# Factors of the output multiplied out in the input projection, and a two-step finish of the head tiles on GpSimd

## What is computed

```
xm, o_pre = split(x @ w_in)                    # 2 x 2048 wide
xc = silu(causal_dwconv(xm, conv_w, conv_b))   # width 4
q, k = headwise(xc, w_q), headwise(xc, w_k);  v = headwise(xm, w_v)
h, C, n, m = mlstm_cell(q, k, v, gates, C, n, m)
hn = (h - mean(h)) * rsqrt(var(h) + eps)       # over the 512 values of a head
out = sigmoid(o_pre) * (hn * norm_g + skip * xc)
y = out @ w_down
```

## Time and profile before

| what | value |
|---|---|
| median of 3 runs | 3442.8 us (3435.66 to 3448.84) |
| the profiled execution | 3447.66 us, of which its span 3446.1 us |
| mean granted TensorE clock | 0.972 of full speed |
| busy, share of the span | TensorE 93%, VectorE 42%, ScalarE 24%, GpSimd 24% |
| projection, loop of it | 1300 to 1650 us |
| score loops of heads 0 to 3 | 1755 to 1876, 1943 to 2067, 2134 to 2258, 2323 to 2443 us |
| down projection | from 2458 us |

### The profile page before, as it was taken

The page is one execution under the profiler, slowest core; times in us unless marked ns, Lnnn a source line. Parts: engine busy times, 40 slices in busy tenths (PEclk is TensorE's granted clock), DMA queues, the critical chain, the costliest instruction groups (busy, mean ns, idle before and its releaser), DMA issues.

```text
span 3446.1 us, 53547 instructions
## 1 busy us (share of the span) xinstructions
PE 3210.0 (93%) x21153; PEld 2934.7 (85%) x21153; DVE 1439.9 (42%) x2086; ACT 813.7 (24%) x1526; POOL 810.4 (24%) x519
## 2 busy tenths in 40 slices
PE   6999899999999989999688879897799999999996
PEld 5777689999999979999476767676799999999995
DVE  2001444333333353433456574748524533333334
ACT  3101532111111151111424233333202311111113
POOL 2112033333323213322001010101232333333320
PEclk9999999999999999999799999999899999999998
DMA  7544211111111104232435353525711111111111
GB/s 214 132 116 111 81 50 50 50 43 49 43 49 43 43 25 175 101 116 81 154 124 205 118 180 132 185 87 186 262 44 44 49 44 49 43 49 43 49 31 51
DMA packets 275684, 318.22 MB, mean 92 GB/s; under 512 B 23577, under 2 KB 215337, under 8 KB 274322
## 3 DMA queue, kind: packets, MB, share of 16 engines
q1 hardware_dynamic: 255289, 250.27, 23.7%
q10 hardware_dynamic: 12960, 40.04, 3.0%
q0 software_dynamic: 7296, 25.96, 2.1%
HBM read 224.88 MB, written 92.19 MB: 92 GB/s over the span
## 4 chain that ended last, share of the span: by engine, by line
PE 82%; DVE 9%; ACT 4%; issue 3%; DMA 2%; SPq 0%; DVEq 0%; ACTq 0%; POOL 0%; POOLq 0%
PE ps L366 22%; PE ps L367 21%; PE ps L368 21%; PE ps L1784 3%; PE ps L1039 2%; PE ps L1002 2%; PE ps L1014 1%; PE ps L1011 1%; PE ps L984 1%; ACT X L448 1%; PE ps L1012 1%; PE ps L1097 1%; DVE DN L1433 1%; PE ps L387 1%; DVE RST L435 1%
## 5 line engine op out<-in xcount | busy, mean ns | idle before, releaser
L366 PE MATMUL ps<-AH,WH 128*128 128x352 f32 x3072 | 1001.7, 326 | 10.3 <-DVE AL L2241 6.2
L367 PE MATMUL ps<-AL,WH 128*128 128x352 f32 x3072 | 987.5, 321 | 0.0
L368 PE MATMUL ps<-AH,WL 128*128 128x352 f32 x3072 | 987.3, 321 | 0.0
L353 POOL TENSOR_SCALAR WH<-RAW 128x1024 fp32r<-128x1024 f32 x200 | 233.0, 1165 | 1748.2 <-PEq L373 1676.5
L366 PEld LDWEIGHTS ps<-AH,WH 128*128 128x128 f32 x3072 | 578.7, 188 | 36.7 <-issue 23.5
L367 PEld LDWEIGHTS ps<-AL,WH 128*128 128x128 f32 x3072 | 580.1, 189 | 0.9
L368 PEld LDWEIGHTS ps<-AH,WL 128*128 128x128 f32 x3072 | 578.0, 188 | 0.0
L355 POOL TENSOR_TENSOR WL<-RAW,WH 128x1024 fp32r<-128x1024 f32 x200 | 506.5, 2533 | 16.7
L366 PE MATMUL ps<-HH,WH 128*128 128x352 f32 x1536 | 500.4, 326 | 0.0
L367 PE MATMUL ps<-HL,WH 128*128 128x352 f32 x1536 | 493.6, 321 | 0.0
L368 PE MATMUL ps<-HH,WL 128*128 128x352 f32 x1536 | 493.2, 321 | 0.0
(11 more groups left out here) (290 smaller groups left out, 3640.0 us busy)
## 6 DMA issues: line engine op xcount, KB each, us to landing
RAW<-in_ffn_w SPq DMA_DIRECT2D x128, 512.0 KB, 3.6
CT<-in_state_mlstm_C SPq DMA_DIRECT2D x32, 1024.0 KB, 5.5
out_C_s<-CT SPq DMA_DIRECT2D x32, 1024.0 KB, 4.6
RAW<-in_ml_w_in SPq DMA_DIRECT2D x32, 512.0 KB, 3.8
RAW<-in_conv_w_pw SPq DMA_DIRECT2D x24, 512.0 KB, 7.4
STK<-u_scratch SPq DMA_DIRECT2D x48, 190.0 KB, 3.5
xc_scratch<-XC ACTq DMA_DIRECT2D x16, 528.0 KB, 2.7
so_scratch<-SO ACTq DMA_DIRECT2D x16, 528.0 KB, 3.7
```

The source lines that it names most:

```text
L353: pool.tensor_scalar(WH[:, k % 4], RAW[:, k % 2], 1.0, 0.0, ALU.mult, ALU.add).then_inc(w_hi, 1)
L366: pe.matmul(ps[:, bank, 0:CW], wh[:, k, cols], hi[:, k, cs], start=(k == 0), stop=False)
L367: pe.matmul(ps[:, bank, 0:CW], wh[:, k, cols], lo[:, k, cs], start=False, stop=False)
L368: mm = pe.matmul(ps[:, bank, 0:CW], wl[:, k, cols], hi[:, k, cs], start=False, stop=(k == nk - 1))
```

## The change

`gate_sigmoid` becomes `silu_tile`: ScalarE applies Silu to XC in place, and VectorE's product goes. A new `out_factors` on VectorE then makes ZT = XC * skip * SO, in one operation, and SO = SO * norm_g in another. It stands in VectorE's queue ahead of the taps of the next tile. `spill_tile` waits for both and writes ZT to a new scratch array too: five DMAs, ahead of XC's. With these, out = hn * (norm_g * SO) + ZT, so `gain` goes, and `finish` is a product and a sum of whole tiles of four feature tiles each (128 x 1024), without a choice of column. GpSimd does it for chunks 0, 1 and 2, and for DEC and END of a head at the start of the next; those of head 3 stay on VectorE. `xo_load` reads ZT's array in place of XC's.

The diff, cut to its core:

```diff
-        def gate_sigmoid(act, j, s):
+        def silu_tile(act, j, s):
             wait(act, mtaps, 8 * j + 8)
-            wait(act, xc_done, j)
-            act.activation(SGX[:], XC[:, s], ACT.Sigmoid).then_inc(sgx_done, 1)
+            act.activation(XC[:, s], XC[:, s], ACT.Silu).then_inc(xc_done, 1)
 
         def spill_tile(act, j, s):
 
             wait(act, xc_done, j + 1)
-            wait(act, so_done, 3 * j + 3)
+            wait(act, z_done, j + 1)
+            act.dma_start(ZS[j], ZT[:]).then_inc(spill[s], 16)
             act.dma_start(XCS[j], XC[:, s]).then_inc(spill[s], 16)
...
+        def out_factors(dve, j, s, stored):
+
+            wait(dve, xc_done, j + 1)
+            wait(dve, so_done, 3 * j + 3)
+            wait(dve, spill[1 - s], stored)
+            dve.scalar_tensor_tensor(ZT[:], XC[:, s], PRM[:, j, 6:7], SO[:, s], ALU.mult, ALU.mult)
+            dve.tensor_scalar(SO[:, s], SO[:, s], PRM[:, j, 5:6], None, ALU.mult).then_inc(z_done, 1)
+
         def phase_a_dve(dve, i, first):
             for s in range(2):
                 j = 2 * i + s
+                if not (first and s == 0):
+                    out_factors(dve, j - 1, 1 - s, 0 if first else 80 * i)
                 dve.wait_ge(xm_put, 4 if first and s == 0 else 3 * j + 3)
...
-                dve.wait_ge(mtaps, 8 * j + 8)
-                dve.wait_ge(sgx_done, j + 1)
-                dve.tensor_tensor(XC[:, s], XC[:, s], SGX[:], ALU.mult).then_inc(xc_done, 1)
...
-            for m, src in enumerate((XCS, SOS)):
+            for m, src in enumerate((ZS, SOS)):
...
+            if not (isinstance(h, int) and h == 0):
+                finish(pool, h - 1, DEC)
+                out_store(pool, h - 1, DEC)
             xo_load(pool, h, 1)
             if not (isinstance(h, int) and h == 0):
+                finish(pool, h - 1, END)
                 out_store(pool, h - 1, END)
...
             vm(4)
+            finish(pool, h, 0)
             out_store(pool, h, 0)
             vm(5)
             xo_load(pool, h, 2)
             vm(6)
+            finish(pool, h, 1)
             out_store(pool, h, 1)
             vm(7)
             xo_load(pool, h, 3)
+            finish(pool, h, 2)
             out_store(pool, h, 2)
             xo_load(pool, h, 4)
-            out_store(pool, h, DEC)
...
-                finish(dve, h - 1, DEC)
...
-            if not first:
-                finish(dve, h - 1, END)
...
-                    if n == 6:
-                        skip(dve, h, tc)
-                    if n == 7:
-                        gate(dve, h, tc)
...
-        def finish(dve, h, tc):
-            skip(dve, h, tc)
-            gate(dve, h, tc)
-
-        def skip(dve, h, tc):
+        def finish(eng, h, tc):
+
+            def absorb():
+                if not isinstance(h, int):
+                    eng.sem_inc(steps_seen, 1)
             w = TC[tc][1]
...
             x = HT[tc % 2][:, :, 0:w]
+            eng.wait_ge(xo_in[tc % 2], (96, 64)[tc % 2] * h + 32 * (tc // 2 + 1))
+            absorb()
+            eng.wait_ge(hnorm, 5 * h + tc + 1)
+            absorb()
+            eng.tensor_tensor(x, x, XO[tc % 2][:, 1, :, 0:w], ALU.mult).then_inc(hskip, 1)
+            eng.wait_ge(hskip, 5 * h + tc + 1)
+            absorb()
+            eng.tensor_tensor(x, x, XO[tc % 2][:, 0, :, 0:w], ALU.add).then_inc(hout, 1)
...
             pool.wait_ge(upd_mm, 4 * DEC_B * HEADS)
+            out_store(pool, HEADS - 1, DEC)
             pool.wait_ge(o_out[1], 16 * 8)
...
-            gain(act, HEADS - 1, DEC)
             down_high(0)
...
+            out_factors(dve, NJ - 1, 1, 80 * NJ // 2)
             dve.wait_ge(t_g, 1)
```

More of the change, by code:

```diff
@@ L270, in program @@
         ma_mm, xm_put, so_done, km_done = sem("ma_mm"), sem("xm_put"), sem("so_done"), sem("km_done")
[L271 removed]
+        gate_mm, gs_put, ge_ev, mtaps, z_done, xc_done = sem("gate_mm"), sem("gs_put"), sem("ge_ev"), sem("mtaps"), sem("z_done"), sem("xc_done")
         mhist_put = sem("mhist_put")
@@ L295, in program @@
         den_abs, den_div, num_ev = sem("den_abs"), sem("den_div"), sem("num_ev")
-        hmean, hcent, hsq, hvar, hsd, hrst, hnorm, hgain, hskip, hout = [sem("h" + x) for x in
-                                                                        ("mean", "cent", "sq", "var", "sd", "rst", "norm", "gain", "skip", "out")]
+        hmean, hcent, hsq, hvar, hsd, hrst, hnorm, hskip, hout = [sem("h" + x) for x in
+                                                                        ("mean", "cent", "sq", "var", "sd", "rst", "norm", "skip", "out")]
         chunk_in = [sem(f"chunk_in{c}") for c in range(3)]
@@ L815, in phase_a_act @@
                 act.wait_ge(gate_mm, j - 1)
-                act.wait_ge(spill[s], 64 * i)
+                act.wait_ge(spill[s], 80 * i)
                 act.sem_inc(steps_seen, 1)
@@ L833, in phase_a_dve @@
                     dve.wait_ge(gate_mm, j - 1)
-                    dve.wait_ge(spill[s], 64 * i)
+                    dve.wait_ge(spill[s], 80 * i)
                 hist = mdec(XM[:, s, MHIST + SEQ:XW], 7)
@@ L1150, in root @@
             act.activation(SD[:, 0:w], ps[:, 7, 256:256 + w], ACT.Sqrt, bias=eps[:]).then_inc(hsd, 1)
-        def gain(act, h, tc):
-            w = TC[tc][1]
-            act.wait_ge(hnorm, 5 * h + tc + 1)
-            if not isinstance(h, int):
-                act.sem_inc(steps_seen, 1)
-            for vt in range(VT):
-                x = HT[tc % 2][:, vt, 0:w]
-                ins = act.activation(x, x, ACT.Copy, scale=PRM[:, hd(h, vt), 5])
-            ins.then_inc(hgain, 1)
         def phase_b_act(act, h, first):
@@ L1179, in phase_b_act @@
                     root(act, h - 1, DEC)
-                if not first and x == 14:
-                    gain(act, h - 1, DEC)
             if first:
@@ L1202, in phase_b_act @@
                     act.activation(DDR[:], DDR[:], ACT.Exp, bias=CC[0:NDEC, 8, bass.ds(h, 1)]).then_inc(ddec, 1)
-                if i == 3 and not first:
-                    gain(act, h - 1, END)
             def high(q):
@@ L1235, in phase_b_act @@
                         root(act, h, tc)
-                    if n == 6:
-                        gain(act, h, tc)
                 if q + 1 < NS:
@@ L1585, in _ @@
             sp.dma_start(NRW[:], a["state_mlstm_n"][0].rearrange("b h (v p) -> (b h v) p", p=P)).then_inc(s_m0, 16)
-            sp.wait_ge(spill[0], 16 * 4 * 8)
-            sp.wait_ge(spill[1], 16 * 4 * 8)
+            sp.wait_ge(spill[0], 16 * 5 * 8)
+            sp.wait_ge(spill[1], 16 * 5 * 8)
             sp.dma_start(XCH[:], inner_tiles(XCS, 0)).then_inc(ld_xc, 16)
@@ L1712, in _ @@
             pool.memset(QZ[:], 0.0).then_inc(s_neg, 1)
-            pool.wait_ge(spill[0], 16 * 4 * 8)
-            pool.wait_ge(spill[1], 16 * 4 * 8)
+            pool.wait_ge(spill[0], 16 * 5 * 8)
+            pool.wait_ge(spill[1], 16 * 5 * 8)
             pool.wait_ge(w_free, NP_A + 32)
@@ L2119, in _ @@
             down_high(1)
-            gain(act, HEADS - 1, END)
             down_high(2)
@@ L2318, in _ @@
             dve.wait_ge(e_cc, 1)
-            dve.wait_ge(spill[0], 16 * 4 * 8)
-            dve.wait_ge(spill[1], 16 * 4 * 8)
+            dve.wait_ge(spill[0], 16 * 5 * 8)
+            dve.wait_ge(spill[1], 16 * 5 * 8)
             block_weights(dve, 0)
```

20 lines of the change are left out of this document (5 added, 15 removed).

## The result

The changed kernel took 3456.76 us (median of 8 runs, 3452.7 to 3460.97); the kernel before took 3443.4 us on the same chip (8 runs, 3435.66 to 3448.84). The ratio is 1.0039, 95% interval 1.0028 to 1.0051: slower by 0.4%, less than the 0.5% that was called within reach of a measurement, but well outside the interval, and 20.8 us above the forecast of 3436.0 and just outside its range.

What follows compares the result with a forecast made beforehand. TensorE was taken as full in the projection; in the score loop TensorE and VectorE wait for each other. Terms +1.1 - 3.2 + 1.6 - 4.5 - 1.8 make -6.8 us: 3436.0 us against the median, range 3420 to 3455.

Steps and rivals of the forecast that it cites:

- The projection: Input projection: added products, fifth store and table loads are covered while TensorE is fully busy; 0 us.
- Rival C: Input projection: ScalarE's table loads are exposed, up to 20.5 us; +13.7 us in all, 3456.5 us; chance 0.04.
- Behind the last tile: After the last projection tile: gate values GE wait for two products and five DMAs; +1.1 us.
- Chunk 0: Score loop, four heads: GpSimd's product delays PL by 0.8 us, less 1.6 for the skip; -0.8 us each.
- Rival B: Chunks 0 and 1: GpSimd's two products back to back shut VectorE out of both; 3451.6 us without clock loss; chance 0.17.
- Chunk 1: Score loop, four heads: mean of PL first (-1.0) and PL late (+1.8); +0.4 us each.
- the late outcome: Chunk 1: PL waits for GpSimd's first product, DN for its second operation; +1.8 us.
- Chunk 2: Score loop: the skip is followed by a 2.40 us wait for TensorE's scores, so nothing to gain; 0 us.
- Between heads: Head turns: gate leaves VectorE's queue, -3.3 us; gain and DEC's finish go from in front of VL, -1.2 us.
- The tail: After the last head: DEC keeps its finish on VectorE but without the gain; -1.8 us.
- its costlier half: Rival B with TensorE's clock halving behind longer waits, about 1.5 us in each of eight places: 3463.6 us; chance 0.09.

Runs made afterwards that it cites:

- e4: The changed kernel with GpSimd's product and sum of chunks 0 and 1 moved one mask later (behind VM 5 and VM 7): 3464.92 us, ratio 1.0059.
- e2: The kernel before plus two idle differences on GpSimd, which read SBUF, in chunks 0 and 1 of each head: 3464.05 us, ratio 1.0053.
- e3: The kernel before plus five idle fills on GpSimd, which read no SBUF operand, in chunks 0 and 1: 3448.01 us, ratio 1.0003.
- e9: The changed kernel with GpSimd's product of chunks 0 and 1 ahead of the mask, sum behind it, chunk 1's sum also awaiting DN: 3433.24 us, ratio 0.9965.
- e8: The changed kernel with six idle instructions ahead of VectorE's loop over the heads: 3462.6 us, ratio 1.0060.
- e1: The changed kernel with product and sum of every chunk, DEC and END on VectorE, GpSimd keeping stores and loads: 3452.5 us, ratio 1.0027.
- e5: e1 with eight idle instructions on VectorE ahead of its head loop: 3439.58 us, ratio 0.9995.
- e7: e5 with only chunk 2, DEC and END finished by GpSimd: 3436.92 us, ratio 0.9980.
- e12: The kernel before with only the last tile's XC store ahead of gate values GE, its other stores behind the row computations: 3444.64 us, ratio 1.0003.

## Why the prediction was wrong

**The projection, 0: right.** TensorE is busy 342.00 of 342.00 us, two products and a fifth store included. The load of a table on ScalarE:

```profile
1506.83 1.28 ACT L763 ACT_TABLE_LOAD   x1
1508.12 1.08 ACT L763 ACTIVATE XC<-XC 128x1056 f32<-128x1056 f32 x1
1510.16 0.46 ACT L782 COPY XM<-ps 128x352 f32<-128x352 f32 x1 [0.96 <-PE ps L369]
```

The Silu follows its load at once, and the wait behind it fell from 2.38 us to 0.96, by about one load. Rival C is out. The price of some 2.66 us a switch that the Trainium skill gives ("ScalarE: Activation LUTs", section "What ACT_TABLE_LOAD costs") doesn't hold here: a load is 1.28 us, and the Silu starts 0.01 us behind it.

**Behind the last tile, +1.1: mis-sized,** +1.9. GE comes 6.4 us behind the Silu where it came 4.6 behind the Sigmoid, +1.8. ZT took 1.32 and SO 0.77 us, as assumed (1.26 and 0.8); the five stores held ScalarE for 4.29 us, from 1650.61 to 1654.90, where 3.58 were assumed.

**Chunk 0, -0.8 each: this step failed,** with +1.8, +2.5, +2.5, +1.5. The mechanism was named (a product of GpSimd shuts VectorE's out for its length), and its price per product was right: 2.37 us on GpSimd, 2.6 to 2.8 on VectorE. What was wrong was what stands there. The prediction saw PL alone, caught by the first product, and the sum beside PSUM readers. But PS stands ahead of PL and is caught too, and PL then by the sum. Rival B had just that pair of 2.4 us, with +1.6 a chunk, and was given a chance of 0.17 in all, because the start of GpSimd's product seemed a race of 0.3 us. e4 showed that behind a mask it is none: one matmul starts both sides, and GpSimd arrives with PS, in all of the eight places.

**Chunk 1, +0.4 each: the same step, the late outcome.** It was a mean of -1.0 and +1.8, and the late one came: 1.3 to 2.0. Its size was right by another pair: PL, which was to be late, went through at 0.41 us, and what the first operation held was the COPY to PS that the prediction had left out, the second DN.

**Chunk 2, 0: nearly right,** -0.1 to -0.6 each. The next PT is not earlier, it comes when TensorE's scores are there, after a wait of 2.40 us before and 2.30 now, although PL was held for 2.59 us here too:

```profile
2250.07 0.29 DVE L1334 TENSOR_TENSOR PT<-ps,DT 128x128 f32<-128x128 f32 x1 [2.30 <-PE ps L1053]
```

The CT ahead of it is some 1.6 us earlier, since the PT in front of that no longer waits for DT behind the gain (1.87 us before); nothing in the loop waits for this CT, so it saves nothing.

**Between heads, -4.5: hit, in part by luck,** -4.6 (-1.8, -3.8, +1.0). The matmul that waited 1.73 us for HT is not the head's first, as the prediction has it: the trace has six ahead of it, and the first of them waits too. That wait for HT is gone at the second and third turn, as was meant, but TensorE's own pause ahead of the six, of unchanged code, grew. Before and after, where head 2 turns into head 3:

```profile
2251.93 3.73 PE L984 MATMUL ps<-XCH,BD 128*128 128x352 f32 x6 [1.24 <-issue]
```

```profile
2257.51 3.88 PE L998 MATMUL ps<-XCH,BD 128*128 128x352 f32 x6 [4.27 <-issue]
```

At these two turns this pause ran from 0.7 to 4.4 us over the kernels here, and no run tells why.

**The tail, -1.8: nearly right,** -1.5. It would have been more: the last store of DEC goes out earlier, and that moves GpSimd's split of the next weight panel onto VectorE's sum, for which TensorE waits (8.24 us); before, it came just after. VectorE and GpSimd:

```profile
2461.12 2.44 DVE L1443 TENSOR_TENSOR SQH<-SQH 128x256 f32<-128x256 f32 x1
```

```profile
2460.63 2.65 POOL L356 TENSOR_TENSOR WL<-RAW,WH 128x1024 fp32r<-128x1024 f32 x1
```

**The whole.** By number rival C's 3456.5 was nearest, by chance, since its table loads cost nothing. By mechanism it was B, with 3451.6, and part of its costlier half: the granted clock over head 2's loop window did not fall (0.93 before, 0.94 after), but only because it was low elsewhere before; behind the wait of chunk 1 it was 0.50 to 0.58 in all four heads, and behind that of chunk 0 in two. There a head's twelve products start 0.21 us apart instead of 0.12, some 1.1 us a place (an estimate from these rows), of which other waits cover a part. The failing terms are chunk 0 (11.6 us off) and chunk 1 (5.4), with the way behind the last tile (0.8) and the tail (0.3); chunk 2 (-1.8) and the heads (-0.1) went the other way: 16.2, from -6.8 to +9.4. That the shut-out carries the loss in the loops is shown by e2 against e3, and by e9, which only reorders GpSimd's queue and adds a wait to it.

The Trainium skill had the rule that decides ("SBUF — State Buffer", section "Who interferes with whom": reads of two SBUF inputs on VectorE and a reading GpSimd exclude each other, a GpSimd write doesn't, and a VectorE copy in its two-port mode contends too). The runs agree on the first two: 0.42 us became 2.6 to 2.8 beside a product and stayed 0.42 beside fills. The COPY's 2.69 us fits the third, though no row tells its mode. It was read and cited, and then applied to one operation instead of to all that stood there.

## What to carry to other kernels

Before work is given to GpSimd that reads SBUF, list each VectorE operation with two SBUF inputs, and every SBUF copy, that stands within its length, and ask what releases each side: where one event starts both, the clash happens every time and is no matter of chance. Then place it beside VectorE's PSUM readers; here putting the product ahead of a mask instead of behind it turned 0.4% slower into 0.35% faster, although one head of four still clashed. When two traces are lined up, take for a mark an operation that somebody waits for. And before a difference of a few tenths of a per cent is believed, look at the waits for nothing at the loops' turns: eight idle instructions were worth 11 us.

## What the runs showed of the hardware that was not expected

- A COPY of 128x256 f32 with a single SBUF input was shut out by GpSimd's product as well, 2.69 us for 0.29. Access passes from one engine to the other instruction by instruction: between product and sum the VectorE operation that had been held was finished, PS in chunk 0 and the COPY in chunk 1, and there PL got through behind it, with the sum at 2.51 us for 2.35.
- The mask VM, with one SBUF input on GpSimd, took 1.11 us instead of 0.69 in e9, beside PS and PL: GpSimd is slowed too where VectorE's operations come first. In head 0, where the mask came first, PL took 3.24 us beside mask and sum.
- VectorE can stall a second time at a loop's turn, 5.15 us for nothing shown, and a shift by eight instructions takes that away. The Trainium skill tells of such a stall ("Runtime: NRT & Kernel Launch", section "Instruction fetch mechanics": a jump to code outside the two pages at hand must fetch it first). That the shift removed it agrees; that e8's shift brought none doesn't help it, and the cause stays open.
- With the finish of chunks 0 and 1 on VectorE, TensorE waits more for the load of the next CT: 2.6 us before, 7.3 in e1, 11.7 in e5, 10.4 in e7. In e9, which is no slower than these, it is 3.2. That this load bounds further gains isn't shown.
- TensorE's clock can be at its lower level without a long wait ahead. In e9 it was 0.50 from 1861 to 1874 us, with TensorE busy for all of these 13.00 us and no wait above 2.0 us in the loop ahead of it; chunk 2 of head 0 became 4.5 us longer than in before. The same happened in head 1 of e9 (4.0 us) and of e12 (3.9).
